# Four chains for the compressed branch, retention scores by pairs, gate columns on the values' step, high part of y first

## What is computed

```
h = rms_norm(x, mix_norm[l])
proj = h @ w_in[l]
gm_u, gm_v, r_q, r_k, r_v, r_g, n_q, n_kv, n_g = jnp.split(proj, splits, axis=-1)
y_a = gmlp_mixer(gelu(gm_u), gelu(gm_v), ...)
y_b = retention_mixer(r_q, r_k, r_v, r_g, ...)      # 4 heads of 64, chunks of 128 tokens
y_c = nsa_mixer(n_q, n_kv, n_g, cmp_pos, cmp_w1, cmp_w2)
...
def compress(t, pos, w1, w2):                        # for keys and for values: 30 blocks x 2048
    ...
    return jax.nn.gelu(flat @ w1) @ w2               # hidden width 128
gates = jax.nn.sigmoid(gate_logits)                  # the 24 columns n_g
```

## Time and profile before

| | |
|---|---|
| median of 3 runs | 1913.28 us (1913.23 to 1913.3) |
| the profiled execution | 1913.26 us, span 1911.5 us |
| busy: TensorE, VectorE, ScalarE, GpSimd | 99%, 71%, 44%, 6% |
| matmuls | 10822 |
| read from memory | 343.02 MB |

### The profile page before, as it was taken

One profiled execution on the slowest core, in us unless ns is written; L12 is line 12 of the kernel. 1 busy time (PEld: TensorE's weight loads), 2 busy tenths in 40 slices (PEclk: granted clock), 3 DMA queues, 4 the chain that ended last, 5 costly groups with the idle time before them and its releaser, 6 DMA issues.

```text
span 1911.5 us, 28527 instructions
## 1 busy us (share of the span) xinstructions
PE 1893.7 (99%) x10822; PEld 1635.5 (86%) x10822; DVE 1359.0 (71%) x1721; ACT 843.0 (44%) x1041; POOL 123.8 (6%) x153
## 2 busy tenths in 40 slices
PE   9999999999999999999999999999999999999998
PEld 9998888888888888888888888888888897888887
DVE  5677777786777767774786677777776668777767
ACT  5554344564334534443354433343344335544333
POOL 1002100320000100000200100000000020010000
PEclk9999999999999999999999999999999999999999
DMA  7424555425555655544444465565555444355553
GB/s 302 177 89 148 194 197 189 152 89 216 198 195 183 261 190 193 182 152 176 168 141 155 169 216 197 181 254 202 194 181 180 143 167 167 132 198 189 196 186 121
DMA packets 48741, 345.29 MB, mean 181 GB/s; under 512 B 5472, under 2 KB 5504, under 8 KB 8720
## 3 DMA queue, kind: packets, MB, share of 16 engines
q1 hardware_dynamic: 43488, 313.02, 45.7%
q0 software_dynamic: 5168, 31.07, 4.4%
HBM read 343.02 MB, written 1.05 MB: 180 GB/s over the span
## 4 chain that ended last, share of the span: by engine, by line
PE 65%; ACT 1%; DVE 1%; issue 0%; POOL 0%; DVEq 0%; POOLq 0%; ACTq 0%
PE bank L1027 16%; PE bank L843 12%; PE bank L845 12%; PE bank L844 12%; PE bank L1026 7%; PE bank L902 1%; PE bank L1132 1%; PE bank L1029 1%; PE bank L1327 1%; PE bank L1106 1%; ACT whi L1506 0%; DVE ysp L1985 0%; PE bank L1358 0%; PE bank L1385 0%; ACT y L1542 0%
## 5 line engine op out<-in xcount | busy, mean ns | idle before, releaser
L1961 DVE TENSOR_TENSOR wlo<-raw,whi 128x2048 fp32r<-128x2048 f32 x294 | 675.6, 2301 | 231.5 <-ACT whi L1506 230.5
L1506 ACT ACTIVATE whi<-raw 128x2048 fp32r<-128x2048 f32 x295 | 563.0, 1910 | 274.2 <-PE bank L845 264.2
L1027 PE MATMUL bank<-ysp,whi 128*128 128x512 f32 x1920 | 666.0, 397 | 0.0
L1026 PE MATMUL bank<-ysp,wlo 128*128 128x256 f32 x1680 | 468.7, 279 | 0.0
L1027 PEld LDWEIGHTS bank<-ysp,whi 128*128 128x128 f32 x1920 | 348.1, 188 | 67.0
L1026 PEld LDWEIGHTS bank<-ysp,wlo 128*128 128x128 f32 x1680 | 316.7, 189 | 10.7
L1589 ACT ACTIVATE sg<-sg 128x256 f32<-128x256 f32 x120 | 50.1, 418 | 466.8 <-DVE sg L2158 466.8
L843 PE MATMUL bank<-whi,ysp 128*128 128x512 f32 (+2 forms) x648 | 237.8, 367 | 3.8 <-DVE ysp L1985 3.2
L845 PE MATMUL bank<-whi,ysp 128*128 128x512 f32 (+2 forms) x648 | 232.5, 359 | 0.0
L844 PE MATMUL bank<-wlo,ysp 128*128 128x512 f32 (+2 forms) x648 | 232.2, 358 | 0.0
L843 PE MATMUL bank<-whi,hl 128*128 128x512 f32 x528 | 206.1, 390 | 0.0
(11 more groups left out here) (334 smaller groups left out, 2347.0 us busy)
## 6 DMA issues: line engine op xcount, KB each, us to landing
raw<-stream SPq DMA_DIRECT2D x296, 1024.0 KB, 4.8
sr<-side POOLq DMA_DIRECT2D x10, 1024.0 KB, 6.5
gbc<-gains POOLq DMA_DIRECT2D x11, 512.0 KB, 3.9
cw<-small POOLq DMA_DIRECT2D x2, 2048.0 KB, 10.6
gbias<-gate_rows POOLq DMA_DIRECT2D x6, 512.0 KB, 3.7
dbias<-dilb POOLq DMA_DIRECT2D x1, 2304.0 KB, 13.9
lng<-rows POOLq DMA_DIRECT2D x2, 1024.0 KB, 5.1
tab<-second POOLq DMA_DIRECT2D x1, 1724.0 KB, 16.1
```

Of the source, the lines that this page charges most:

```text
L1026: pe.matmul(o[:, 0, :], lo[:, k, cols], yh[:, k, :], start=False, stop=False, skip_group_check=True)
L1027: last = pe.matmul(o, hi[:, k, cols], ysp[:, :, k, :], start=k == 0, stop=k == 7)
L1506: act.activation(whi[s], raw[s], ACT.Copy).then_inc(hi_made, 1)
L1961: dve.tensor_tensor(wlo[s], raw[s], whi[s].bitcast(F32), ALU.subtract).then_inc(lo_made, 1)
```

## The change

1. `compressed_hidden` goes through k in eight rounds of four products: keys and values, first and second half of the 16 weight blocks, each on its own 32 columns of the array and its own 32 partitions of bank 2 (`tile_position`). ScalarE copies the second halves (partitions 64 to 125), VectorE adds the first, then ScalarE applies gelu. `hidden_T` is one transpose.
2. `retention_scores(2)` and `(3)` stand together behind `retention_out(1)`.
3. The 24 gate columns move to the values' step. Its tile holds 7 x 128 rows of 280 columns; the last 128 rows (`kxr`) come by a DMA of their own and are split beside. Old step 12 and `gates_T` go away, one tile of each layer too. The values' step is two steps with a bank each. The sigmoid is made later, exp on ScalarE, the rest on VectorE. Queries are now steps 12 and 13, keys 14, values and gates 15 and 16, and the retention norm stands behind the drain of 13.
4. `first_half` and `opening_step` wait for `yh` alone, do the products with it, and wait for `yl` before the last ones. `keep_warm(12, 5)` becomes `keep_warm(6, 5)`.
5. In `beside(1)` the copy goes ahead of the rotation.

```diff
--- before.py
+++ after.py
-WIN_DRAINS = "AADDAADDAAAAADDDD"
-PLAN2.led_by_pair("win", WIN_DRAINS[:2], WIN_DRAINS[2:], 4)
+WIN_DRAINS = "AADDAADDAAAADDDDD"
+PLAN2.led_by_pair("win", WIN_DRAINS[:2], WIN_DRAINS[2:15], 4)
+PLAN2.more(WIN_DRAINS[15:], 2)
...
+                if l == 0:
+                    pool.wait_ge(x_scaled, 4)
+                pool.dma_start(kxr, one(small, l)[:, 4772:4772 + GATE_N]).then_inc(kx_in, 16)
...
-                return {(0, 0): lambda: copied(B, tb + 1), (0, 4): lambda: copied(B, tb + 2),
+                return {(0, 0): lambda who: copied_by(B, tb + 1, who), (0, 4): lambda who: copied_by(B, tb + 2, who),
...
+                t = slice(0, P)
+                for q in range(2):
+                    if q:
+                        pe.wait_ge(side_hi, B.side(stage) + 1)
+                        pe.wait_ge(side_lo, B.side(stage) + 1)
+                        hi, lo = side_of(stage)[0::2]
+                    else:
+                        tile_split(B, tile)
+                        hi, lo = whi[B.slot(tile)], wlo[B.slot(tile)]
+                    late[(0, 4 * q)]("A")
+                    for k in range(4):
+                        c = slice(512 * k, 512 * k + 512)
+                        if k and (0, 4 * q + k) in late:
+                            late[(0, 4 * q + k)]()
+                        pe.matmul(pb[0], yh[:, 4 * q + k, t], lo[:, c], start=q == 0 and k == 0, stop=False)
+                        pe.matmul(pb[0], yh[:, 4 * q + k, t], hi[:, c], start=False, stop=False)
+                    late[(0, 4 * q)]("D")
+                    for k in range(4):
+                        c = slice(512 * k, 512 * k + 512)
+                        last = pe.matmul(pb[0], yl[:, 4 * q + k, t], hi[:, c], start=False, stop=q == 1 and k == 3)
+                last.then_inc(row_done, 1)
...
-            keep_warm(12, 5)
+            keep_warm(6, 5)
...
+                    for q in range(2):
+                        copied_by(B, 2 * m + q + 1, "A")
+                        for k in range(4 * q, 4 * q + 4):
...
+                            pe.matmul(pb[0][:, 256 * m:256 * m + 256], yh[:, k, t], hi[:, k, :], start=k == 0, stop=False)
+                        copied_by(B, 2 * m + q + 1, "D")
+                        for k in range(4 * q, 4 * q + 4):
...
-                    for kv in range(2):
-                        for lp in range(16):
-                            last = pe.matmul(pb[2][0:30, kv * P:kv * P + P], blk[:, kv, lp, :, :].rearrange("p g n -> p (g n)"),
-                                             cw1[:, kv, lp, :], start=lp == 0, stop=lp == 15)
+                    for j in range(8):
+                        n = 30 if j else 32
+                        for half_ in range(2):
+                            for kv in range(2):
+                                r, lp = 64 * half_ + 32 * kv, 8 * half_ + j
+                                cols = blk[:, kv].rearrange("p l g n -> p (l g n)")[:, 30 * lp:30 * lp + n]
+                                last = pe.matmul(pb[2][r:r + n, 0:P], cols, cw1[:, kv, lp, :], start=j == 0, stop=j == 7, tile_position=(0, r))
...
-                def gates_T():
-                    pe.wait_ge(drain_act, B.drained(plan.step["win"] + 13, "A"))
-                    keep_warm(1, 2)
+                def values_and_gates():
+
+                    tile = plan.tile["win"] + 14
+                    tile_split(B, tile)
+                    pe.wait_ge(kx_lo, l + 1)
+                    sl = B.slot(tile)
+                    hi, lo = rows3(whi[sl], 7, GATE_N), rows3(wlo[sl], 7, GATE_N)
                     for m in range(M):
-                        last = pe.transpose(pb[2][:, 24 * m:24 * m + 24], ngT[0:24, m * P:m * P + P], ident[0:24, 0:24])
-                    last.then_inc(ngt_done, 1)
+                        bank_free(B, plan.step["win"] + 15 + m, False)
+                        t = slice(m * P, m * P + P)
+                        for k in range(KC):
+                            last = three(pb[1 - m][:, 0:GATE_N], (yh[:, k, t], yl[:, k, t]), (hi[:, k, :], lo[:, k, :]) if k < 7 else (kxh, kxl),
+                                         k == 0, k == KC - 1)
+                        last.then_inc(step_done, 1)
...
-                        if i <= 11:
-                            retention_scores(i - 8)
-                    if i == 14:
-                        gates_T()
+                        if i == 11:
+                            retention_scores(2)
+                            retention_scores(3)
+                values_and_gates()
...
+                    if i == 12:
+                        load_table(ACT.Exp)
+                        act.wait_ge(kx_in, 16 * (l + 1))
+                        act.activation(kxh, kxr, ACT.Copy).then_inc(kx_hi, 1)
...
                     if i == 6:
                         act.wait_ge(hid_done, l + 1)
-                        act.activation(hidT[0:30].rearrange("p i c -> p (i c)"), pb[2][0:30, 0:2 * P], ACT.Gelu_apprx_tanh).then_inc(hid_act, 1)
+                        act.activation(hidT[0:62, :], pb[2][64:126, 0:P], ACT.Copy).then_inc(hid_half, 1)
+                    if i == 7:
+                        act.wait_ge(hid_sum, l + 1)
+                        act.activation(hidT[0:62, :], hidT[0:62, :], ACT.Gelu_apprx_tanh).then_inc(hid_act, 1)
+                act.wait_ge(drain_dve, B.drained(plan.step["win"] + 17, "D"))
+                ngf = ng.rearrange("p m g r b -> p (m g r b)")
+                act.activation(ngf, ngf, ACT.Exp, scale=-1.0).then_inc(ng_exp, 1)
...
                 if i == 1:
+                    heads_copied(2)
                     turn(3)
-                    heads_copied(2)
...
-                    ahead(B, "win", i - 1)
+                    if i < 16:
+                        ahead(B, "win", i - 1)
+                    if i == 6:
+                        dve.wait_ge(hid_half, l + 1)
+                        dve.tensor_tensor(hidT[0:62, :], pb[2][0:62, 0:P], hidT[0:62, :], ALU.add).then_inc(hid_sum, 1)
+                    if i == 12:
+                        dve.wait_ge(kx_hi, l + 1)
+                        dve.tensor_tensor(kxl, kxr, kxh.bitcast(F32), ALU.subtract).then_inc(kx_lo, 1)
...
-                            ins = dve.tensor_copy(nv, o)
+                            dve.tensor_copy(nv[:, i - 15, :], pb[i % 2][:, 0:256])
+                            ins = dve.tensor_copy(ng[:, i - 15].rearrange("p g r b -> p (g r b)"), pb[i % 2][:, 256:GATE_N])
...
-                    if i == 14:
+                    if i == 13:
...
-                    if i == 15:
-
-                        dve.wait_ge(ngt_done, l + 1)
-                        ngf = ng.rearrange("p m g r b -> p (m g r b)")
-                        link(dve.tensor_scalar(ngf, pb[2][:, 0:48], 1.0, None, ALU.add))
...
                 dve.wait_ge(kc_ready, l + 1)
                 dve.tensor_tensor(bd[0:120], bdrow.unsqueeze(1).broadcast_to([120, HN, 64]), bc(blockm[0:120, :], 64), ALU.mult).then_inc(bd_ready, 1)
                 dve.wait_ge(cs_ready, M * (l + 1))
+                dve.wait_ge(ng_exp, l + 1)
+                ngf = ng.rearrange("p m g r b -> p (m g r b)")
+                link(dve.tensor_scalar(ngf, ngf, 1.0, None, ALU.add))
+                link(dve.reciprocal(ngf, ngf))
...
-        tiles.append(weight_tile([part(3456, P), part(3712, P)], D))
+        tiles.append(weight_tile([values_gates(w)[:7 * P]], 7 * P))
```

More of the change, by code:

```diff
@@ L49 @@
 LAYERS = 2
+GATE_N = 256 + 24
 class Plan:
@@ L153 @@
 SIDES = PLAN1.sides + LAYERS * PLAN2.sides + 1
-assert PLAN2.tiles % 3 == 0 and len(PLAN2.copies) % 2 == 0
+assert len(PLAN2.copies) % 2 == 0
 GATE_BANKS = (1, 0, 1) + (0,) * 9
@@ L481, in build @@
         ng = at("ng", L2 + 800, M * 24, shape=(M, 2, 4, 3))
-        ngT = at("ngT", A + 94 * K, S)
+        kxr = at("kxr", A + 72 * K, GATE_N)
+        kxl = at("kxl", A + 72 * K, GATE_N, F32R)
+        kxh = at("kxh", A + 74 * K, GATE_N, F32R)
         bdrow = at("bdrow", A + 13 * K + 512, 64)[0:120, :]
@@ L931, in token_pair @@
                         bank_free(B, step + m, beside)
+                    if m == 0 and late:
+                        first_half(B, stage, tile, late)
+                        continue
                     t = slice(m * P, m * P + P)
                     for k in range(KC):
[L934 to L937, removed]
+                        if m == 0 and k % 4 == 0:
                             tile_split(B, tile + k // 4)
@@ L1340, in hidden_T @@
                     keep_warm(1, 3)
-                    for kv in range(2):
-                        last = pe.transpose(pb[3][:, kv * 30:kv * 30 + 30], hidT[0:30, kv, :], ident[0:30, 0:30])
-                    last.then_inc(hidt_done, 1)
+                    pe.transpose(pb[3][:, 0:62], hidT[0:62, :], ident[0:62, 0:62]).then_inc(hidt_done, 1)
                 def compressed_kv():
@@ L1388, in layer @@
                 token_pair(B, "win", 0, plan.tile["win"], True, norm_late(B, "n5", 6 + 3 * l))
```

(7 more changed lines are left out.)

58 lines of the change are left out of this document (30 added, 28 removed).

## The result

The changed kernel takes 1892.77 us (median of 4 runs, 1892.62 to 1892.87), the kernel before 1913.29 us in the same comparison. The ratio is 0.9893, with a 95% interval of 0.9878 to 0.9907: 20.5 us less. The forecast was 1892.1 us, between 1889.5 and 1897.5. The head of the page, busy time first, answers to the earlier trace rows.

What follows compares the result with a forecast made beforehand. TensorE, busy 99% of the span, was taken as the bound. Savings of 10.4 (hidden products), 2.0 (retention scores), 3.8 (gate columns), 3.9 (norms), 0.1 (opening) and 1.0 (grouped attention) sum to 21.2 us: 1892.1 us, range 1889.5 to 1897.5.

## What to carry to other kernels

Small products with few output columns, as the hidden ones here, are bound by the distance of passes on one column part (0.109 us); put four chains on four parts and alternate them in the program, for TensorE went past only three waiting passes of a part. When a wait goes away, read every engine's queue up to the next meeting point: an engine with no gap there is the next bound, and a new order inside it may only move the wait, as it did here. A norm's wait for another engine is a place for a split; and a wait of TensorE can make the products behind it slower, by 0.08 us for the next one and by the granted clock after a long one, so read both before pricing it.

## What was not expected of the hardware

- Passes waiting for one column part are passed over by those of another up to three deep: the next chain started 5 to 6 ns behind the thirteenth of sixteen passes, with one chain ahead of it and with two.
- After TensorE's scores of 15 columns and an idle time of 2.34 us the granted clock was 0.50 for 6.8 us in one layer and 3.4 us in the other, which added 2.8 and 1.55 us to the wait; behind the wait of 1.19 us between the values' half steps it stayed at 1.00.
- A VectorE operation on 4 columns of 128 partitions took 0.17 us alone, 0.17 when it started between 5 ns behind and 4 ns ahead of a GpSimd product, and 0.72 to 0.74 when it started 12 to 31 ns behind it.
- Behind a wait of TensorE the second product starts later than in a run of products: 0.31 us in place of 0.23 for 512 columns, 0.21 in place of 0.13 for 280, 0.19 in place of 0.12 for 256.
